# Memory attention of a ten-stage transformer kernel: product banks taken in turn, queries multiplied in their bank, two query tiles per step

## The reference, cut to what matters

```python
def memory_cross_attention(h, m, w_q, w_kv, w_o):
    q = (h @ w_q).reshape(B, S, N_XHEADS, XHEAD_DIM)
    k, v = jnp.split(m @ w_kv, 2, axis=-1)          # both (B, M, N_XHEADS, XHEAD_DIM)
    s = jnp.einsum('bshd,bmhd->bhsm', q, k) * (XHEAD_DIM ** -0.5)
    p = jax.nn.softmax(s, axis=-1)
    o = jnp.einsum('bhsm,bmhd->bshd', p, v).reshape(B, S, D_MODEL)
    return o @ w_o
x = x + memory_cross_attention(rmsnorm(x, g_xattn), rmsnorm(mem, g_mem), w_xq, w_xkv, w_xo)
```

## Time and profile before

| what | value |
|---|---|
| median of 3 runs | 3242.61 us (3242.28 to 3246.74) |
| the profiled execution | 3238.06 us |
| its span, first to last instruction | 3236.0 us |
| PE (matmuls) busy | 3020.8 us, 93%, x14864 |
| DVE / ACT / POOL busy | 1525.1 / 1078.4 / 839.5 us |
| mean granted TensorE clock | 0.962 |
| chain that ended last | PE 79%, DVE 9%, ACT 5%, POOL 3% |

### The profile page before, as it was taken

One profiled execution on the slowest core, in us unless ns is written; L12 is line 12 of the kernel. 1 busy time (PEld: TensorE's weight loads), 2 busy tenths in 40 slices (PEclk: granted clock), 3 DMA queues, 4 the chain that ended last, 5 costly groups with the idle time before them and its releaser, 6 DMA issues.

```text
span 3236.0 us, 36194 instructions
## 1 busy us (share of the span) xinstructions
PE 3020.8 (93%) x14864; PEld 2497.8 (77%) x14864; DVE 1525.1 (47%) x2241; ACT 1078.4 (33%) x1704; POOL 839.5 (26%) x470
## 2 busy tenths in 40 slices
PE   7999999888999999999999889999987988888898
PEld 6888888777888888888887777888876676676777
DVE  4554254633455435553354434455325445446663
ACT  3232244333332223322343333333232333233442
POOL 2000244443200010000444543000043443254442
PEclk8999999999999999999999899999997999889999
DMA  3332232222233233322321322332321111021111
GB/s 126 98 98 91 85 83 69 69 94 79 89 100 96 94 100 96 98 93 96 86 66 53 104 89 75 98 98 88 104 77 46 46 37 49 27 66 59 52 58 47
DMA packets 289588, 257.23 MB, mean 79 GB/s; under 512 B 10871, under 2 KB 288272, under 8 KB 289424
## 3 DMA queue, kind: packets, MB, share of 16 engines
q1 hardware_dynamic: 289104, 254.90, 25.3%
q0 software_dynamic: 320, 0.03, 0.0%
HBM read 252.79 MB, written 2.10 MB: 79 GB/s over the span
## 4 chain that ended last, share of the span: by engine, by line
PE 79%; DVE 9%; ACT 5%; POOL 3%; issue 3%; DMA 1%; SPq 0%; ACTq 0%; DVEq 0%; POOLq 0%
PE PS L1333 25%; PE PS L1334 24%; PE PS L1335 24%; PE PS L1339 2%; ACT WH L1698 1%; POOL WL L2536 1%; PE PS L1587 1%; PE PS L1421 1%; DVE AR L2161 1%; ACT SC L1856 1%; DVE AF L2439 1%; POOL RAW L2522 1%; DVE AR L2177 0%; DVE SC L2397 0%; DVE SM L2244 0%
## 5 line engine op out<-in xcount | busy, mean ns | idle before, releaser
L1333 PE MATMUL PS<-XH,WL 128*128 128x512 f32 x2256 | 911.8, 404 | 13.8 <-issue 8.9
L1335 PE MATMUL PS<-XH,WH 128*128 128x512 f32 x2256 | 888.9, 394 | 0.0
L1334 PE MATMUL PS<-XL,WH 128*128 128x512 f32 x2256 | 887.8, 394 | 0.0
L1698 ACT ACTIVATE WH<-RAW 128x1024 fp32r<-128x1024 f32 x448 | 465.3, 1043 | 1024.8 <-PE PS L1335 1003.9
L2059 DVE TENSOR_TENSOR WL<-RAW,WH 128x1024 fp32r<-128x1024 f32 (+1 forms) x296 | 374.2, 1267 | 519.0 <-ACT WH L1698 505.0
L2536 POOL TENSOR_TENSOR WL<-RAW,WH 128x1024 fp32r<-128x1024 f32 x184 | 448.8, 2446 | 560.0 <-ACT WH L1698 533.2
L1333 PE MATMUL PS<-AR,WL 128*128 128x512 f32 (+1 forms) x1216 | 477.2, 392 | 53.6 <-DVE SC L2155 24.4
L1333 PEld LDWEIGHTS PS<-XH,WL 128*128 128x128 f32 x2256 | 429.9, 191 | 98.0 <-issue 11.4
L1335 PEld LDWEIGHTS PS<-XH,WH 128*128 128x128 f32 x2256 | 428.7, 190 | 93.1
L1334 PEld LDWEIGHTS PS<-XL,WH 128*128 128x128 f32 x2256 | 430.4, 191 | 81.6 <-issue 1.9
L1334 PE MATMUL PS<-AR,WH 128*128 128x512 f32 (+1 forms) x1216 | 470.1, 387 | 0.0
(11 more groups left out here) (251 smaller groups left out, 3419.5 us busy)
## 6 DMA issues: line engine op xcount, KB each, us to landing
RAW<-in_w_ffn_gu_dram SPq DMA_DIRECT2D x176, 512.0 KB, 3.5
RAW<-in_w_ffn_down_dram SPq DMA_DIRECT2D x80, 512.0 KB, 3.4
RAW<-in_w_mix_in_dram SPq DMA_DIRECT2D x48, 512.0 KB, 3.8
RAW<-in_w_xkv_dram SPq DMA_DIRECT2D x32, 512.0 KB, 3.3
RAW<-in_a_w_in_dram SPq DMA_DIRECT2D x32, 512.0 KB, 3.7
RAW<-in_w_mix_out_dram SPq DMA_DIRECT2D x16, 512.0 KB, 3.4
RAW<-in_w_xq_dram SPq DMA_DIRECT2D x16, 512.0 KB, 3.3
RAW<-in_w_xo_dram SPq DMA_DIRECT2D x16, 512.0 KB, 3.3
```

The source lines that it names most:

```text
L1333: pe.matmul(o, ll, rh, start=start, stop=False, skip_group_check=skip)
L1334: pe.matmul(o, lh, rl, start=False, stop=False, skip_group_check=skip)
L1335: return pe.matmul(o, lh, rh, start=False, stop=stop, skip_group_check=skip)
L1698: act.activation(h, src, ACT.Copy).then_inc(sg["wh"].up(n))
```

## The change

The memory attention is rewritten and its steps get functions of their own (`keys`, `vals`, `queries`; `xke`, `xve`, `xqe`; `xs`, `xn`, `xt`; `xkl`, `xvl`, `xql`, `xtl`, `xpl` for the low halves).

- Banks 0 to 3 are taken in turn by all products: both key tiles go in one bank (256 columns each), the values take one, each query tile one, each `xpv` one. Products go column tile by column tile, no longer alternating between two banks.
- Queries are multiplied by `RB` in their bank; ACT and the low half read the bank, which is free after the low half.
- Low halves are put in the list 3 or 4 product-counts after the high half; the scaling of the weights (`xn`) 6 after its scores.
- Attention goes in steps of two query tiles: one bank for two score tiles, one maximum over both, one scaling of both with a broadcast, transposes through banks 6 and 7 in turn. Scores begin 16 product-counts into the next head.
- A weight unit's slot is freed at the second column tile's last product that uses it.
- The output product is woven with the last head's attention at a rate of 8.2 steps in 48 counts.

Only the memory stages use what is changed; the functions shared with the differential layer are split off from it and do there what they did.

```diff
-PACE = {"mm": 1, "vmm": 0.5, "score": 1, "dscore": 1, "tr": 0.5, "bs": 1.5, "ms": 2, "bt": 1, "bpv": 2.5, "mpv": 2.5, "dpv": 2, "xpv": 2}
+PACE = {"mm": 1, "vmm": 0.5, "xs": 2, "xt": 1, "dscore": 1, "tr": 0.5, "bs": 1.5, "ms": 2, "bt": 1, "bpv": 2.5, "mpv": 2.5, "dpv": 2, "xpv": 2}
...
@@ -625,64 +625,80 @@
         self.post(s + 1, (6, 7))
 
     def xattn(self, s):
+
+        self.own_banks(0, 1, 2, 3)
+        self.watch = lambda n: None
+        for h in range(4):
+            self.chunk((s, f"k{h}"), [None, None], "m", [None, ("el", (s, "k", h))], n=256)
+            self.chunk((s, f"v{h}"), [None], "m", [("vl", (s, h))])
+            self.chunk((s, f"q{h}"), [None, None], "x", [("el", (s, "q", h, c)) for c in range(2)])
+
+        def keys(h):
+            ch = ((s, f"k{h}"), 0)
+            b = self.take()
+            for c in range(2):
+                yield from self.tile(ch, b, c)
+            self.give(b)
+            self.add("xke", (s, h), "eh", at=(s, "k", h))
+            self.later(4, "xkl", (s, h), "el", at=(s, "k", h))
+
+        def vals(h):
+            b = self.take()
+            yield from self.rows_tile(((s, f"v{h}"), 0), 0, b)
+            self.give(b)
+            self.add("xve", (s, h), "vh")
+            self.later(4, "xvl", (s, h), "vl")
+
+        def queries(h):
+            for c in range(2):
+                b = self.take()
+                yield from self.tile(((s, f"q{h}"), 0), b, c)
+                self.give(b)
+                self.add("xqe", (s, h, c), "et", "eh", at=(s, "q", h, c))
+                self.later(4, "xql", (s, h, c), "el", at=(s, "q", h, c))
+
         def att(h):
-            for n in range(6):
-                if n >= 2:
-                    self.add("tr", (s, 4 * h + n - 2), "ptr", "ph", "pl")
-                    yield
-                if n < 4:
-                    self.add("score", (s, 4 * h + n), "score", "nbias", "exps", "prob")
-                    yield
+
+            yield
+            for step, low in (("xkl", (s, h)), ("xvl", (s, h)), ("xql", (s, h, 0)), ("xql", (s, h, 1))):
+                self.due(step, low)
+            for r in (2 * h, 2 * h + 1):
+                self.add("xs", (s, r), "score", "nbias", "exps")
+                self.later(6, "xn", (s, r), "prob")
+                yield
+            yield
+            for r in (2 * h, 2 * h + 1):
+                self.due("xn", (s, r))
+                self.add("xt", (s, r), "ptr", "ph")
+                self.later(3, "xtl", (s, r), "pl")
+                yield
+            for r in (2 * h, 2 * h + 1):
+                self.due("xtl", (s, r))
             for d in range(2):
-                self.add("xpv", (s, 2 * h + d), "pv", "yh", "yl")
+                b = self.take()
+                self.bank_of[s, 2 * h + d] = b
+                self.add("xpv", (s, 2 * h + d), "pv", "yh")
+                self.give(b)
+                self.later(4, "xpl", (s, 2 * h + d), "yl")
                 yield
 
-        def evk(ch):
-            for c in range(2):
-                self.add("evk", (ch, c), "eh", "el")
-                yield
-
-        def evq(ch):
-            for c in range(2):
-                self.add("evq", (ch, c), "et", "eh", "el")
-                yield
-
-        side = self.stream(iter(()), 1)
-        pend = self.stream(iter(()), 1)
-        for h in range(4):
-            ck = ((s, f"k{h}"), 0)
-            self.chunk((s, f"k{h}"), (0, 1), "m", [("el", (ck, c)) for c in range(2)], n=256)
-            cv = ((s, f"v{h}"), 0)
-            self.chunk((s, f"v{h}"), (4,) if h == 0 else (2,), "m", [("vl", (cv, 0))])
-            cq = ((s, f"q{h}"), 0)
-            self.chunk((s, f"q{h}"), (2, 3) if h == 0 else (0, 1), "x", [("et", (cq, c)) for c in range(2)])
-            self.weave(self.mm(ck), side, pend)
-            self.finish(pend)
-            if h == 0:
-                self.add("barrier", (s,))
-            kp = self.stream(evk(ck), 0.3)
-            self.weave(self.vmm(cv, 2), side, kp)
-            self.finish(kp)
-            if h == 0:
-                self.norm_a(s)
-            self.add("evh", (cv, 0), "vh")
-            self.add("evl", (cv, 0), "vl")
-            gq = self.mm(cq)
-            if h == 0:
-                for _ in range(8):
-                    next(gq)
-                self.norm_b(s)
-            self.weave(gq, side)
+        self.drain(self.flow(keys(0)))
+        self.add("barrier", (s,))
+        self.drain(self.flow(vals(0)))
+        self.norm_a(s)
+        g = queries(0)
+        for _ in range(8):
+            next(g)
+        self.norm_b(s)
+        self.drain(self.flow(g))
+        for h in range(1, 4):
+            side = self.stream(att(h - 1), 8.2 / 64)
+            self.weave(self.flow(self.chain(keys(h), vals(h), queries(h))), side)
             self.finish(side)
-            pend = self.stream(evq(cq), 0.3)
-            next(pend[0])
-            next(pend[0])
-            side = self.stream(att(h), 0.18)
-        self.finish(pend)
-        side[1] = 0.3
-        self.out_proj(s, side)
-
-    def out_proj(self, s, side):
+        self.own_banks(4, 5)
+        self.out_proj(s, self.stream(att(3), 8.2 / 48), flow=True)
+
+    def out_proj(self, s, side, flow=False):
         def out(p, bb):
             return self.chunk((s, f"o{p}"), (bb, bb + 1), "o", [("x", (s + 1, 2 * p + c)) for c in range(2)])
 
...
+        self.weave(self.flow(early()) if flow else early(), side)
         self.finish(side)
+        self.tick(99)
         self.drain(g)
...
             self.add("mm", (ch, c, i), "mm")
-            if i == len(C.kmap) - 1 and c == C.cols - 1:
+            if c == C.cols - 1 and (i == len(C.kmap) - 1 or C.kmap[i + 1][0] != C.kmap[i][0]):
                 self.retire((ch, c, i))
...
                 self.ready(C.kmap[k][0])
                 self.add("vmm", (ch, i, k), "mm")
-                if i == 3 and k == KT - 1:
+                if n == len(C.banks) - 1 and i % 2 and k == KT - 1:
                     self.retire((ch, i, k))
...
-                if over:
+                o = c * C.n if C.n < T else 0
+                mm3(PS[b][:, o:o + C.n], h[:, kk, cs], l[:, kk, cs], rh, rl, i == 0, over).then_inc(sg["mm"].up(ch, c, i))
+                if over and C.frees[c] is not None:
                     g, key = C.frees[c]
                     free[b] = [sg[g].at(*key)]
 
...
+            def xs(s, r):
+                h, b = r // 2, 4 + r % 2
+                bank_free(b)
+                qh, ql = x_queries(h)
+                kh, kl = x_keys(h)
+                on.wait_ge(*sg["el"].at(s, "k", h))
+                for d in range(2):
+                    on.wait_ge(*sg["el"].at(s, "q", h, d))
+                for i in range(2):
+                    qs = slice(256 * (r % 2) + 128 * i, 256 * (r % 2) + 128 * i + 128)
                     for d in range(2):
+                        t = mm3(PS[b][:, 256 * i:256 * i + 256], qh[:, d, qs], ql[:, d, qs], kh[:, d, :], kl[:, d, :], d == 0, d == 1)
+                t.then_inc(sg["score"].up(s, r))
+                free[b] = [sg["exps"].at(s, r)]
+            def xt(s, r):
+                b = 6 + r % 2
+                p = x_row(r)
+                on.wait_ge(*sg["prob"].at(s, r))
+                bank_free(b)
+                for j in range(2):
+                    for i in range(2):
+                        o = 256 * j + 128 * i
+                        t = pe.transpose(PS[b][:, o:o + 128], p[:, i, 128 * j:128 * j + 128], ID)
+                t.then_inc(sg["ptr"].up(s, r))
+                free[b] = [sg["pl"].at(s, r)]
...
             def xpv(s, n):
                 h, d = divmod(n, 2)
-                bank_free(7)
-                on.wait_ge(*sg["vl"].at(((s, f"v{h}"), 0), 0))
-                on.wait_ge(*sg["pl"].at(s, 4 * h + 3))
+                b = P.bank_of[s, n]
+                bank_free(b)
+                on.wait_ge(*sg["vl"].at(s, h))
+                on.wait_ge(*sg["pl"].at(s, 2 * h + 1))
                 vh, vl = v_place(s, h)
                 ds = slice(d * 128, (d + 1) * 128)
                 for j in range(2):
-                    t = mm3(PS[7][:, :], vh[:, j, ds], vl[:, j, ds], PX[:, j, :], PX[:, 2 + j, :], j == 0, j == 1)
+                    t = mm3(PS[b][:, :], vh[:, j, ds], vl[:, j, ds], PX[:, j, :], PX[:, 2 + j, :], j == 0, j == 1)
                 t.then_inc(sg["pv"].up(s, n))
-                free[7] = [sg["yl"].at(s, n)]
...
+            def xke(s, h):
+                C = chunks[(s, f"k{h}"), 0]
+                on.wait_ge(*sg["mm"].at((C.name, 0), 1, KT - 1))
+                if h > 1:
+                    on.wait_ge(*sg["score"].at(s, 2 * h - 3))
+                act.activation(x_keys(h)[0], PS[C.banks[0]].rearrange("p (c t) -> p c t", c=2), ACT.Copy).then_inc(sg["eh"].up(s, "k", h))
+            def xqe(s, h, c):
+                C = chunks[(s, f"q{h}"), 0]
+                on.wait_ge(*sg["et"].at(s, "q", h, c))
+                if h > 1:
```

(44 more changed lines are left out.)

## The result

The changed kernel takes 3184.68 us in the median of four runs (3182.23 to 3190.33); the kernel before, run beside it, 3242.45 us (3239.68 to 3246.74). The ratio is 0.9823, with a 95% interval of 0.9805 to 0.9841: 1.8% faster. The forecast was 3192 us with a range of 3182 to 3210.

The account below looks back on a forecast made before the run. The order of DVE's list, not its amount of work, was taken to hold PE. Heads 42.0, output-product wait 12.9, last wait +0.6, new wait -3.8, starts -0.5: 51 us off 3242.61 gives 3192, range 3182 to 3210.

Parts of the forecast that it names:

- heads (periods without a wait): Heads of both memory stages: 29.4 us each without waits, losing 7.1 and 6.9 before; 42.0 us gained in all.
- wait ahead of the output product, its slow clock, L2272: Before the output product: 3.65 us wait, 0.3 restart, 2.5 slow clock, twice, 12.9 gained; last value product's wait, 0.6 more.
- new wait there: As the output product begins, its fixed banks were just used: new wait of 1.9 us a stage, bounds 0.5 and 4.
- starts: Start of both memory stages: waits on POOL's low half stay; zero gain, bounds -2 and +9, entered as -0.5 us.
- the prediction's rule: Whole sum: leave clock ramps out, dropping some 11 us over both stages; gain 40 us, time 3202.
- (a): Rival, within heads: value products wait 1 us at each of 16, output product 3 us; 3210 us, chance 0.10.
- (b): Rival, stage starts: their waits go too, about 8 us a stage; 3176 us, chance 0.06.
- (c): Rival, bank takes: each waits for DVE's low half and the clock falls; 3302 us at 2.5 a take, chance 0.03.
- (d): Rival, each head: a weight unit is late by one POOL subtraction, 2.4 us x 8 = 19; 3211 us, chance 0.05.

Follow-up runs that it names:

- the first ladder: Three edits put into the kernel before in four combinations: list order alone 3221.26 us, banks in turn alone 3248.87, order and later scores 3200.19, all three 3201.82.

## Why the prediction was right

By its terms, in us of the profiled executions, both stages together:

| term | forecast | measured |
|---|---|---|
| heads (periods without a wait) | 42.0 | 44.4 |
| wait ahead of the output product, its slow clock, L2272 | 13.5 | 14.3 |
| new wait there | -3.8 | -3.3 |
| starts | -0.5 | -0.9 |
| memory stages | 51.2 | 54.5 |
| all else | 0 | -3.4 |
| span | 51 | 51.1 |

Measured heads: (109.53 - 3 x 28.99) + (108.82 - 3 x 28.98). Output product: 57.45 and 57.55 us before, 50.36 and 50.35 after. New wait: the third period is 1.67 longer than the second. Starts: head 0 went from 35.06 to 35.03 and from 33.58 to 34.50. The last but one line is code that the change does not reach, 5.2 us of it behind the second stage; that the total hit 51 within a few tenths is a small error of one sign and a small scatter of the other.

**The cause was the right one.** "The order of DVE's list, not the amount of DVE's work, holds PE" is shown by the first ladder: the order alone takes 3 to 4 us off a period of 36.5, later scores another 2 to 3, the banks in turn at most 0.8. The order is thus enough for about half of the gain. That it is needed is not shown: banks in turn with late scores and the list's old order were not run, nor late scores alone. The last 1.2, from 30.2 to 29.0, comes with the rest of the change. Of it 0.65 are the waits of the transposes; one bank does as well as two, so the fewer and wider steps, or where they stand in the list, removed them. The other 0.5 are shorter PE time for the same products at a clock of 1.00, 28.99 us instead of 29.46: the small breaks around waits and steps, which the profile does not list as waits.

**The mis-sized term** is the head: 29.4 were put and 28.99 measured, for the 0.5 us that I added for short breaks where steps are put between products. The profile shows none; PE is busy for all 28.99. Over six heads that is the 2.4 us between 42.0 and 44.4.

**The new wait** came where it was put, 1.50 us where 1.9 were taken, in both stages. One detail was wrong: I had it on the second query tile's multiply and low half in the second stage, on bank 1. The turn stands at the same place in both stages, so both wait for bank 0 and the last value product's low half. The row of DVE ahead of it, 0.15 us before PE goes on at 763.76:

```profile
762.92 0.69 DVE L2309 TENSOR_TENSOR AR<-PS,AR 128x512 fp32r<-128x512 f32 x1 [1.29 <-ACT AR L1914]
```

**The starts** stayed, as forecast: 9.0 and 8.1 us on POOL WL, where 7 to 9 were put. The slow clock behind the first is in the rows:

```profile
656.40:660.90 4.50, 4.48 (x21) 4.48 (x22) 0.00 (x0) 0.00 (x0) 4.50 (x2) 0.50 0.59 193
```

4.5 us at 0.50 of full speed (1.2 GHz), 2.2 us lost, near the 2.5 that the earlier trace rows gave for a shorter wait. The second stage's start is less even: I put it at zero, and head 0 got 0.9 us longer. In the five kernels whose edits leave that place alone it takes 35.35 to 35.53 us, 1.8 to 1.9 more than before, with 9.0 us of wait for the same row and not 8.1. The -0.9 of the table is the lucky end of that.

**Ramps in the sum.** The Trainium skill ("TensorE: Matmul & The Clock Gate", Part 1) gives the ramp, for modelling, as under 1% of a typical kernel's span, and it speaks there of the warm-up. Taken for recurring waits too, as in the prediction's rule, the forecast would have been 40 us and 3202. The stages gave 54.5. How much of it was slow clock is seen where the same products run at both: the output product of the kernel before and of the one with only the order changed (columns of the earlier trace rows):

```profile
785.28:842.73 57.45, 53.06 (x235) 43.31 (x236) 24.38 (x41) 21.23 (x36) 19.73 (x10) 0.94 0.22 72
```

```profile
774.56:828.75 54.19, 50.98 (x236) 41.55 (x236) 24.24 (x41) 21.11 (x36) 19.74 (x10) 1.00 0.24 75
```

That is 2.1 us, and the three periods ahead of it give 1.5, 1.0 and 1.5 in the same way: 6.1 us in the first stage, small breaks around the waits included, where the rule's 11 us for both had put 5.5. In this kernel, where the same wait comes back at every head, slow clock belongs in the sum.

**The rivals.** (a) Value products that wait for their probabilities: no such row in any stage, even with the low halves undelayed. (b) The starts going too: no, though one moved line in POOL's list brings half of them. (c) Turning banks breaking the stream: the clock in the heads is 1.00. The section "A second HAM failure mode" of the same page tells of a kernel whose clock fell through cycling banks; none of the kernels here that turn banks behave so for that reason; the one at 0.91 had the waits. (d) Late weight units: POOL WL is not awaited in any head.

The median came out 7.3 us under the forecast: the profiled execution before was 4.5 us under its median, that of after 2.0 us over its own, and the medians' difference is 57.8 us.

## What to carry to other kernels

When an engine waits for a buffer, follow the engine that empties it through its own list: a step that waits for a third engine, put ahead of the emptying, costs more than the emptying. Taking away the resource that the wait names gains nothing if the next consumer needs the same late result; look for the first moment at which the late value is wanted, and put products between. Choose the next bank by when its tile ended, not by when it was taken.

## What the runs showed of the hardware

- In the heads and the output product, single waits of 1.5, 2.1 and 2.5 us left the granted clock at 1.00 (the kernel with only the order changed; 1.5 in the changed kernel too). Two waits of 2.1 and 1.1 to 1.3 us, less than 1 us of work apart, put the period's mean at 0.91 (banks in turn). Behind single waits of 3.65 us and 9.0 us the clock was at 0.5. I had priced slow clock by the length of a single wait; two shorter ones close together cost 2.0 us as well.
- A DVE instruction on two columns, 0.17 us alone, took 2.37 us when it met POOL's subtraction, while the same on one column took 0.15 beside it. The Trainium skill, "SBUF — State Buffer", section "Who interferes with whom", says that a DVE instruction in a two-port mode and a GpSimd instruction lock each other out for a whole instruction, and the trace agrees: the held one ends with POOL's. It also has instructions with two SBUF inputs contend. That agrees with the low half from SBUF, 2.41 us beside POOL; in the changed kernel with the queries through SBUF it took 0.68 us beside an idle POOL and 1.51 to 2.48 beside a subtraction; read from a bank it took 0.68 to 0.69 beside either.
- The product with the reciprocals, two SBUF operands, took 0.69 us in all of its eight uses a stage. All sixteen of the two stages ran while POOL was idle, so its upper bound of 2.4 was not tested.
